# Final norm of a hybrid decoder step: root on ScalarE and inverse on VectorE in place of logarithm and exponential, two thirds of the results finished on GpSimd

## What is computed

```
def rmsnorm(x, g):
    xf = x.astype(jnp.float32)
    y = xf * lax.rsqrt(jnp.mean(xf * xf, axis=-1, keepdims=True) + EPS)
    return (y * g.astype(jnp.float32)).astype(x.dtype)
...
    x = x + 0.5 * swiglu(rmsnorm(x, n3), f2g, f2u, f2d)
...
        return rmsnorm(x, final_norm), ...
```

## Time and profile before

| | |
|---|---|
| time, median of 3 runs | 2513.39 us (2512.98 to 2513.55) |
| the profiled execution, its own time | 2514.98 us |
| its span | 2513.2 us |
| busy: PE, DVE, ACT, POOL | 2462.3, 1702.6, 1306.1, 179.4 us |
| granted TensorE clock over the span | 0.996 |

### The profile page before, as it was taken

How to read it: one execution, slowest core, us unless ns; L and a number is a source line. 1 busy time by engine, 2 the same in 40 slices (tenths; PEclk the granted TensorE clock), 3 DMA queues, 4 the chain that set the end, 5 groups by cost and what they waited for, 6 DMA issues and landing times.

```text
span 2513.2 us, 51536 instructions
## 1 busy us (share of the span) xinstructions
PE 2462.3 (98%) x19305; PEld 2421.6 (96%) x19305; DVE 1702.6 (68%) x2879; ACT 1306.1 (52%) x2203; POOL 179.4 (7%) x210
## 2 busy tenths in 40 slices
PE   8999999999998999999999999999999999999997
PEld 7999999999988999999999999999999999999997
DVE  6766667777677777677576766443486677767676
ACT  5355455555466666665656655311444555555554
POOL 0011111111130000000000000000200111111110
PEclk9999999999999999999999999999999999999999
DMA  3345555555631222211321225423113555555555
GB/s 123 111 102 125 126 125 118 122 121 118 180 118 37 76 68 76 68 60 63 117 85 67 101 76 202 146 101 118 32 45 122 123 117 120 123 123 125 125 126 183
DMA packets 78566, 271.06 MB, mean 108 GB/s; under 512 B 8320, under 2 KB 12800, under 8 KB 77952
## 3 DMA queue, kind: packets, MB, share of 16 engines
q1 hardware_dynamic: 55424, 185.11, 21.3%
q0 software_dynamic: 23040, 84.55, 17.7%
HBM read 154.86 MB, written 114.77 MB: 107 GB/s over the span
## 4 chain that ended last, share of the span: by engine, by line
PE 83%; DVE 7%; ACT 3%; DMA 3%; issue 3%; POOL 0%; DVEq 0%; SPq 0%; ACTq 0%; POOLq 0%
PE banks L146 26%; PE banks L147 26%; PE banks L148 26%; DMA raw<-w_slabs 1%; PE banks L1939 1%; DMA x_sum<-f_snap 1%; DMA x_sum<-f_part 1%; DVE b L1657 1%; DVE mix_blk_lo L499 1%; ACT mix_u_hi L1374 1%; PE banks L1734 1%; DVE mix_u_lo L1379 0%; DVE mix_blk_f L475 0%; PE banks L435 0%; DVE mix_sum L1400 0%
## 5 line engine op out<-in xcount | busy, mean ns | idle before, releaser
L146 PE MATMUL banks<-f_blk_hi,f_u_hi 128*128 128x258 f32 x2496 | 708.1, 284 | 5.8 <-DVE f_blk_lo L499 5.0
L147 PE MATMUL banks<-f_blk_lo,f_u_hi 128*128 128x258 f32 x2496 | 706.4, 283 | 0.0
L148 PE MATMUL banks<-f_blk_hi,f_u_lo 128*128 128x258 f32 x2496 | 705.5, 283 | 0.0
L146 PE MATMUL banks<-mix_blk_hi,mix_u_hi 128*128 128x258 f32 x1808 | 526.2, 291 | 5.6 <-DVE vb L1414 2.3
L147 PE MATMUL banks<-mix_blk_lo,mix_u_hi 128*128 128x258 f32 x1808 | 511.5, 283 | 0.0
L148 PE MATMUL banks<-mix_blk_hi,mix_u_lo 128*128 128x258 f32 x1808 | 510.3, 282 | 0.0
L146 PEld LDWEIGHTS banks<-f_blk_hi,f_u_hi 128*128 128x128 f32 x2496 | 472.1, 189 | 8.9 <-DVE f_blk_lo L499 4.0
L148 PEld LDWEIGHTS banks<-f_blk_hi,f_u_lo 128*128 128x128 f32 x2496 | 471.9, 189 | 0.0
L147 PEld LDWEIGHTS banks<-f_blk_lo,f_u_hi 128*128 128x128 f32 x2496 | 471.7, 189 | 0.1
L146 PEld LDWEIGHTS banks<-mix_blk_hi,mix_u_hi 128*128 128x128 f32 x1808 | 342.5, 189 | 12.5 <-issue 7.2
L147 PEld LDWEIGHTS banks<-mix_blk_lo,mix_u_hi 128*128 128x128 f32 x1808 | 342.4, 189 | 3.0
(11 more groups left out here) (282 smaller groups left out, 4370.2 us busy)
## 6 DMA issues: line engine op xcount, KB each, us to landing
raw<-w_slabs SPq DMA_DIRECT2D x220, 512.0 KB, 3.4
x_sum<-f_part POOLq DMA_DIRECT2D x126, 516.0 KB, 7.8
x_sum<-f_snap POOLq DMA_DIRECT2D x18, 516.0 KB, 10.2
x_sum<-x POOLq DMA_DIRECT2D x16, 516.0 KB, 5.7
x<-x_sum SPq DMA_DIRECT2D x16, 516.0 KB, 8.6
sg_kept<-sgt SPq DMA_DIRECT2D x8, 1032.0 KB, 5.7
sgs<-sg_kept SPq DMA_DIRECT2D x16, 516.0 KB, 4.5
x<-x_t SPq DMA_DIRECT2D x8, 516.0 KB, 8.3
```

Source lines behind the costliest of these rows:

```text
L146: pe.matmul(out, wh, xh, start=start, stop=False, skip_group_check=chained)
L147: pe.matmul(out, wh, xl, start=False, stop=False, skip_group_check=chained)
L148: return pe.matmul(out, wl, xh, start=False, stop=stop, skip_group_check=chained)
```

## The change

The final norm alone changes. ScalarE takes the root of the mean (`norm_root`, ACT.Sqrt) in place of the logarithm, and no exponential; VectorE inverts the result (`norm_inverse`, a reciprocal of 128 x 344) behind tile 12, behind tile 20, and before its last five results. Sixteen of the 24 results (all of group 0, m = 0 to 4 of group 1, m = 5 to 7 of group 2: `POOL_TILES`) are made in two steps: ScalarE writes x * gain into y (`norm_scale`), and GpSimd multiplies y by the inverse in place (`norm_apply_gpsimd`). VectorE keeps eight, all behind tile 23. The transfers are nine pieces as before, of other tiles and in another order. The preload of a table for the logarithm goes. The earlier norms wait for the same counts as before (steps=2).

```diff
+POOL_TILES = (range(KT), range(5), range(5, KT))
...
             if m == t:
-                norm_rstd(act, k, s, t - 1)
-                if t == 2:
-                    act.preload_act_table(ACT.Ln)
+                norm_root(act, k, s, t - 1)
+            if m in POOL_TILES[t - 1]:
+                norm_scale(act, k, s, t - 1, m)
+    for m in POOL_TILES[2]:
+        norm_scale(act, k, s, 2, m)
+
+
+def norm_root(act, k, s, t):
+    act.wait_ge(s.mean_ready, t + 1)
+    act.activation(s.rstd[:, tg(t)], k.bank[s.banks[t]][:, 0:TG], ACT.Sqrt, bias=k.eps[:, 0:1]).then_inc(s.rstd_step, 1)
+
+
+def norm_inverse(dve, k, s, t):
+    dve.wait_ge(s.rstd_step, t + 1)
+    dve.reciprocal(s.rstd[:, tg(t)], s.rstd[:, tg(t)]).then_inc(s.inverse, 1)
...
-    pe.wait_ge(s.rstd_step, 3)
+    pe.wait_ge(s.rstd_step, 2)
...
-        pe.wait_ge(s.rstd_step, 2 * t - 1)
+        pe.wait_ge(s.rstd_step, s.steps * (t - 1) + 1)
...
 def norm_apply(dve, k, s, t, m):
 
-    if m == 0:
-        dve.wait_ge(s.rstd_step, 2 * t + 2)
+    dve.wait_ge(s.inverse, s.inverse_base + t + 1)
...
+def norm_apply_gpsimd(pool, k, s):
+
+    scaled = 0
+    for t in range(NT):
+        pool.wait_ge(s.inverse, s.inverse_base + t + 1)
+        for m in POOL_TILES[t]:
+            scaled += 1
+            pool.wait_ge(s.scaled, s.scaled_base + scaled)
+            pool.tensor_tensor(k.y[:, m, tg(t)], k.y[:, m, tg(t)], s.rstd[:, tg(t)], ALU.mult).then_inc(s.h_pool, 1)
+
+
+def norm_scale(act, k, s, t, m):
+
+    act.activation(k.y[:, m, tg(t)], s.x[:, m, tg(t)], ACT.Copy, scale=k.vec[:, s.gain, m:m + 1]).then_inc(s.scaled, 1)
...
-        if 17 <= n < 23:
-            norm_apply(dve, k, s, 0, n - 17)
-    for m in (6, 7):
-        norm_apply(dve, k, s, 0, m)
-    for t in (1, 2):
-        for m in range(KT):
-            norm_apply(dve, k, s, t, m)
+        if n in (12, 20):
+            norm_inverse(dve, k, s, n // 8 - 1)
+    for m in range(5, KT):
+        norm_apply(dve, k, s, 1, m)
+    norm_inverse(dve, k, s, 2)
+    for m in range(5):
+        norm_apply(dve, k, s, 2, m)
...
-            pieces = [(t, m, m + 4) for t in range(NT - 1) for m in (0, 4)]
-            pieces += [(NT - 1, m, n) for m, n in ((0, 2), (2, 4), (4, 6), (6, 7), (7, 8))]
-            for t, m, n in pieces:
-                sp.wait_ge(n3.h_ready, t * KT + n)
+            pieces = [(0, 0, 4, n3.h_pool, n3.pool_base + 4), (0, 4, 8, n3.h_pool, n3.pool_base + 8), (1, 5, 8, n3.h_ready, 3),
+                      (1, 0, 5, n3.h_pool, n3.pool_base + 13), (2, 0, 2, n3.h_ready, 5), (2, 2, 4, n3.h_ready, 7),
+                      (2, 5, 7, n3.h_pool, n3.pool_base + 15), (2, 4, 5, n3.h_ready, 8), (2, 7, 8, n3.h_pool, n3.pool_base + 16)]
+            for t, m, n, ready, count in pieces:
+                sp.wait_ge(ready, count)
```

More of the change, by code:

```diff
@@ L3010, in build @@
                    rstd_at=(2, 4), **n1_tiles)
-        nm = stage("nm", MEAN + " " + HEAD + " " + EARLIER, gain=GMIX, x=k.x1, banks=(5, 5, 7), rstd_at=(5, 6), **nm_tiles)
+        nm = stage("nm", MEAN + " " + HEAD + " " + EARLIER, gain=GMIX, x=k.x1, banks=(5, 5, 7), rstd_at=(5, 6), steps=2, **nm_tiles)
         f1 = stage("f1", FFN, first=SLAB_FFN1, norm=n1, next_norm=nm, x=k.x1, mean_after=(10, 21), **k.ffn1, **ffn(0))
@@ L3021, in build @@
         w.sg_loaded = [sem(f"sg_loaded{n}") for n in range(2)]
-        n2 = stage("n2", MEAN + " " + HEAD + " " + EARLIER, gain=G2, x=k.x, banks=(7, 7, 7), rstd_at=(4, 6), **n2_tiles)
+        n2 = stage("n2", MEAN + " " + HEAD + " " + EARLIER, gain=G2, x=k.x, banks=(7, 7, 7), rstd_at=(4, 6), steps=2, **n2_tiles)
         o = stage("o", "m_hi m_lo unit_ready unit_used", up_ready=w.up_ready, m_ready=w.m_ready, next_norm=n2,
@@ L3025, in build @@
         w.out = o
-        n3 = stage("n3", MEAN + " h_ready", gain=GFIN, x=k.x, banks=(3, 3, 3), **n3_tiles)
+        n3 = stage("n3", MEAN + " h_ready", gain=GFIN, x=k.x, banks=(3, 3, 3), steps=1, h_pool=n2.added,
+                   pool_base=6 * NT, scaled=w.oa_hi,
+                   scaled_base=KT, inverse=w.zeroed, inverse_base=6, **n3_tiles)
         f2 = stage("f2", FFN, first=SLAB_FFN2, norm=n2, next_norm=n3, x=k.x, mean_after=(9, 18), **k.ffn2, **ffn(1))
@@ L3089, in _ @@
             ffn_scalar(act, k, f2)
-            norm_rstd(act, k, n3, 2)
+            norm_root(act, k, n3, 2)
         @block.vector
@@ L3113, in _ @@
             ffn_gpsimd(pool, k, f2)
+            norm_apply_gpsimd(pool, k, n3)
         @block.tensor
```

## The result

The changed kernel takes 2520.32 us (median of 8 runs, 2517.96 to 2523.87), the kernel before 2513.47 us beside it (8 runs, 2511.32 to 2516.69). The ratio is 1.0026 with a 95% interval of 1.0017 to 1.0036: slower by 6.9 us. The prediction was 2517.5 us, so the sign was right, the time lies inside the range and 2.8 us above the number.

What follows compares the result with a forecast made beforehand. VectorE's results and transfers were taken as level at the end. Sixteen results fewer give 7.8 us, three reciprocals cost 6.2, meetings 5.5 (check: +3.9); the time-ordered +4.1 on 2513.39 made 2517.5 us, range 2512.4 to 2520.8.

Steps and rivals of the forecast that it cites:

- The case that I held for true: The time-ordered forecast with each VectorE reciprocal at 1.80 to 2.52 us: 2516.0 to 2519.5 us, chance 0.55.
- the reciprocal at eight times the slope: Rival: each of three VectorE reciprocals takes 2.93 us, adding 2.6 us to the forecast, 2520.1 us; chance 0.17.
- the ports held for the whole instruction: Rival: VectorE and GpSimd alternate wholly at SBUF, nine meetings at 1.44 instead of 1.16 us, +2.5, 2520.0; chance 0.03.
- ScalarE costs nothing: In the final norm, 16 scalings replace table loads and exponentials; square plus scaling takes 0.76 of a tile's 0.95 us.
- The reciprocal: Each of VectorE's three 128 x 344 reciprocals takes 2.05 us, between 1.80 and 2.52 us.
- Both rivals: VectorE's reciprocal takes 0.54 us (no change, 2513.4 us, chance 0.22) or 2.93 us (2520.1 us, chance 0.17).
- The meetings: While GpSimd works, VectorE's addition-and-square-sum pairs and its results take 1.16 us each, against 0.95 and 0.49 alone.
- the sum: Time-ordered path from tile 12 to the span's end: 2517.3 us against 2513.2, so +4.1 us.
- TensorE's wait ahead of the mean of group 1: TensorE idles some 3 us there; the mean starts at 2495.0 instead of 2492.07, at 0.31 us a half pass.
- The end: Third reciprocal done at 2508.1, group 2's result m = 3 at 2512.1, then six tiles to transfer; span ends at 2517.3.
- the last issue of y near 2513: Sign in the final norm's transfers: the last piece of output y is issued near 2513 us.
- the DMA queue empty between 2500 and 2506: Sign in the final norm's transfers: no output data queued from 2500 to 2506 us.

Runs made afterwards that it cites:

- the wait filled: The changed kernel plus fourteen matmuls that nobody reads, run in TensorE's wait ahead of the mean of group 1; 2518.53 us, ratio 1.0019 to the kernel before.
- The squares ahead of the preload: The kernel before, with the logarithm's table preloaded ahead of tile 18's square and a second preload after tile 19's square; 2512.24 us, ratio 0.9989.
- the last experiment: The squares ahead of the preload, plus group 0's results m = 6 and 7 scaled on ScalarE and finished early on GpSimd; 2512.46 us, ratio 0.9990 to the kernel before.
- GpSimd's share alone: The kernel before, its logarithm, exponential and table loads kept, with the changed kernel's 16 results on ScalarE and GpSimd and its transfer order; 2519.49 us, ratio 1.0021.
- the kernel with the later reciprocals: The changed kernel with its first two reciprocals moved behind tile 17's square sum and behind tile 23; 2518.45 us, ratio 1.0014 to the kernel before.

## Why the prediction was right or wrong

**Direction and mechanism: right.** VectorE loses more by three reciprocals and by meeting GpSimd than the 16 results give back. Each half was seen apart: reciprocals without GpSimd +3.76, a meeting without a reciprocal 0.69 us for each GpSimd instruction, and a kernel with no wait of TensorE over 0.73 us and no lower clock still +2.76.

**The range: right by luck.** The case that I held for true had its own range, 2516.0 to 2519.5, and 2520.32 is above it. The time lies inside the wide range only because that was drawn up to 2520.8 for two rivals, the reciprocal at eight times the slope (2520.1) and the ports held for the whole instruction (2520.0), and neither of them came. The median is 0.27% slower (0.17 to 0.36%), so of the two outcomes it is the one to which I gave 0.34, and not "same" with 0.64.

**ScalarE costs nothing: right in this change, and more was hanging on it than I wrote.** Scalings took 0.47 us from start to start between squares at 0.38, so a pair takes 0.85 of the 0.95 us and not 0.76, and no square came late. Where the table loads stay, ScalarE is full with the same scalings, and the last mean starts 2.2 us later into the stage than before (27.95 against 25.74).

**The reciprocal: inside its range, 0.16 us low.** I took 2.05 us, and it is 2.21 from start to start (2.29 in its row). Three of them are 0.5 us of the miss. The 128 x 8 one still takes 203 ns, so a column costs (2295 - 203) / 336 = 6.2 ns over about 153 ns: the reading in which the reciprocal shares the copies' fixed part. Both rivals fall, 0.54 and 2.93 us. The Trainium skill (VectorE: DVE Perf Modes, "First, the fixed hardware budget") has a repeat count of 8 for this operation. Eight times the slope was estimated at 2.93 us; the row says 2.29, which is nearer to six times.

**The meetings: right in their pace, and partly by luck in what they add.** Pairs came at 1.15 us behind a first one of 1.39 (the sum had 1.16, and 0.2 until the two are in step), and the last five results took 4.58 us where the sum had 4.46 (two at 0.49 and three at 1.16). But the sum took 0.95 us as what VectorE needs for a pair, and it needs 0.85. Up to the mean of group 1 the sum therefore had some 1.7 us for the reciprocal and 1.25 for the meetings, and the runs show 1.27 and 1.80. The two errors cancel: 2.93 in all against 3.07. Both were priced from rows of another norm nearly two milliseconds earlier in the program. The whole-instruction lock would show 1.44 us in every pair, and only the first comes near it.

**TensorE's wait ahead of the mean of group 1: right in size, wrong in its price.** I wrote "TensorE idle some 3 us ahead of the mean of group 1" among the signs, measured 3.06, and then priced the matmuls behind it at the full clock: "A half pass is 2.48 / 8 = 0.31 us, so the mean's four end at 2496.25; tile 19's products take 0.95". **This is the step that failed.** The clock was 0.50 through the mean, tile 19 and tile 20, so tile 20's addition stands 2.9 us behind the sum. With the wait filled it stands 0.07 behind. I had no term for it, and no rival. A row that should have made me look was there: the earlier trace rows shows the clock at 0.50 over 2510 to 2512, after TensorE's last work, though with no work behind it on which a price could be read, and though the same rows have it at 1.00 over 2504 to 2506, when TensorE's last work had ended at 2502.66.

**The end: right in length, wrong in places.** From the third inverse to the end of the span I had 9.2 us, measured 8.98. But the signs "the last issue of y near 2513" and "the DMA queue empty between 2500 and 2506" do not hold: the last issue is at 2518.71, and the DMA share is 0.86 over 2500 to 2502 and 0 from 2504 to 2510. Of the 5.7 us by which that issue is later, 1.55 are the later start of the stage and 3.5 the lateness of the third inverse (37.79 against 34.32); the rest, under 1 us, is that two pieces are issued behind VectorE's last result.

The sum with the two corrections is 4.1 + 2.8 + 0.5 = +7.4 against +7.35 in the profiled execution and +6.9 in the medians. That it closes so well is owed in part to the errors above that cancel.

**What stays open.** The squares ahead of the preload gained 0.90 us in the stage and 2.8 us in the medians. The interval of the ratio, 0.9981 to 0.9998, is a gain of 0.5 to 4.8 us and holds 0.9 too, and the change touches nothing ahead of the stage. I take the stage's 0.9 us for the mechanism and don't know whether the rest is more than scatter.

## What to carry to other kernels

Before work goes from VectorE to GpSimd, ask what each GpSimd instruction takes from VectorE, and where. Beside VectorE's results it took 0.69 us for a result that VectorE writes in 0.49; beside pairs of an addition and a sum it took 0.30 (1.15 less 0.85). So a share can pay while VectorE adds tiles, as the last experiment has it in the trace (0.88 us in the stage, not told apart in the ratio), and it does not pay at the end. A wait put on TensorE is not paid with its own length alone; look in the trace at the granted clock behind waits of that length, and if none is there, carry the work behind it at both clocks in the range. And when a table load makes an engine late, try first to move the load past the one instruction that is waited for, as that gained 0.9 us here with two preloads placed anew, where replacing the functions lost 3.8.

## What the runs showed of the hardware

TensorE's granted clock fell to 0.5 (1.2 GHz) after waits of 3.06, 2.64 and 2.45 us in this stage, and held at 1.00 (2.4 GHz) after waits of 0.18 to 1.46 us. In the changed kernel it was low from about 2496 until between 2502 and 2503, most of it with TensorE at work. It need not be low when the work begins: after the wait of 2.45 us the first two half passes still took 0.83 us, and the next eight 4.17 in place of 2.48, as in these windows of GpSimd's share alone:

```profile
2502.00:2504.00 2.00, 2.00 (x5) 1.30 (x6) 2.00 (x4) 2.00 (x6) 1.64 (x2) 0.63 0.00 0
2504.00:2506.00 2.00, 2.00 (x5) 1.08 (x4) 0.50 (x2) 0.62 (x2) 0.00 (x0) 0.51 0.28 106
```

By quarters of a microsecond the clock is 1.00 up to 2502.50 and 0.56 in the next, so it fell some 0.7 us behind the end of the wait (2501.86), with TensorE at work. No wait between 1.46 and 2.45 us was seen in this stage, so which waits do harm is not shown beyond the ones named.

The two engines do not share the loss of a meeting evenly. GpSimd's eight results of group 0 took 8.69 us beside VectorE, 1.09 each, against 1.02 for its three additions alone (3.07 us), while VectorE's results went from 0.49 to about 1.16. And not every instruction of VectorE meets GpSimd: the reciprocal, which has one input, took 2.29 us with GpSimd at work (2500.04 in the kernel with the later reciprocals) as with GpSimd idle (2488.26 in the changed kernel), and the additions of tiles, which read PSUM, kept their 0.50 us.
